# A hybrid decoder block: x fetched turned, its normalisation applied to the products, parameter vectors as one table

## The reference, cut to what matters

```python
def rms_norm(x, g):
    xf = x.astype(jnp.float32)
    y = xf * lax.rsqrt(jnp.mean(xf * xf, axis=-1, keepdims=True) + EPS)
    return (y * g.astype(jnp.float32)).astype(x.dtype)
...
        n = rms_norm(h, g_mix[i])
        proj = n @ w_in[i]
        z = proj[..., :SPLIT_Z]
        xbc = proj[..., SPLIT_Z:SPLIT_XBC]
        dt_raw = proj[..., SPLIT_XBC:SPLIT_DT]
        q = proj[..., SPLIT_DT:SPLIT_Q].reshape(bsz, s, SB_HEADS, SB_HEAD_DIM)
        ...
        gates = jax.nn.sigmoid(proj[..., SPLIT_V:])
```

## Time and profile before

| | |
|---|---|
| median, lowest, highest of three runs | 1225.63, 1223.95, 1225.75 us |
| span of the profiled execution | 1222.8 us (its own time is not given beside it) |
| PE busy | 1161.0 us, 95% |
| DVE, ACT, POOL busy | 302.0, 245.0, 235.6 us |
| DMA, whole span | 451.56 MB, mean 369 GB/s |
| mean granted clock of PE | 0.998 |

### The profile page before, as it was taken

How to read it: one execution, slowest core, us unless ns; L and a number is a source line. 1 busy time by engine, 2 the same in 40 slices (tenths; PEclk the granted TensorE clock), 3 DMA queues, 4 the chain that set the end, 5 groups by cost and what they waited for, 6 DMA issues and landing times.

```text
span 1222.8 us, 15282 instructions
## 1 busy us (share of the span) xinstructions
PE 1161.0 (95%) x6802; PEld 591.8 (48%) x6802; DVE 302.0 (25%) x463; ACT 245.0 (20%) x349; POOL 235.6 (19%) x206
## 2 busy tenths in 40 slices
PE   9999999999999999999999999989999998899996
PEld 9998878998433333333333333333333333333332
DVE  5448363224311221121122112111211211121112
ACT  6486686445101000000000000000000000000001
POOL 6979769882001000000000000000000000000000
PEclk9999999999999999999999999999999999999999
DMA  9644537848899999999999999999999999999994
GB/s 318 209 138 140 171 104 275 318 154 366 369 426 427 421 429 426 437 430 428 429 429 431 435 431 430 428 433 431 430 430 432 429 431 434 429 429 410 428 427 199
DMA packets 44702, 451.56 MB, mean 369 GB/s; under 512 B 4916, under 2 KB 5272, under 8 KB 27736
## 3 DMA queue, kind: packets, MB, share of 16 engines
q1 hardware_dynamic: 44632, 450.54, 88.8%
HBM read 449.48 MB, written 1.05 MB: 368 GB/s over the span
## 4 chain that ended last, share of the span: by engine, by line
PE 62%; DMA 33%; DVE 2%; ACT 1%; issue 1%; POOL 1%; DVEq 0%; ACTq 0%; POOLq 0%
DMA ring<-in_w_down 20%; PE ps L1275 19%; PE ps L1299 12%; PE ps L865 10%; DMA spare_quad<-in_w_down 7%; DMA kv_quad<-in_w_down 6%; PE ps L808 6%; PE ps L1246 3%; PE ps L1321 2%; PE ps L1178 2%; PE ps L829 1%; PE ps L1312 1%; PE ps L1197 1%; PE ps L980 1%; PE ps L889 0%
## 5 line engine op out<-in xcount | busy, mean ns | idle before, releaser
L513 POOL TENSOR_TENSOR w_parts<-ring,w_parts 128x512 fp32r<-128x512 f32 x162 | 216.9, 1373 | 42.0 <-ACT w_parts L1487 33.3
L692 POOL TENSOR_SCALAR ss<-ss 128x1 f32<-128x1 f32 (+2 forms) x8 | 1.5, 191 | 868.9 <-ACT junk L1477 864.5
L1275 PE MATMUL ps<-ring,xs 128*64 128x512 f32 x688 | 151.8, 595 | 5.8 <-DMA ring<-in_w_gu 5.8
L2216 DVE TENSOR_SCALAR xbuf<-ps 128x512 f32<-128x512 f32 x32 | 22.1, 691 | 526.4 <-PE ps L1275 526.4
L1299 PE MATMUL ps<-ring,xbuf 128*64 128x512 f32 x576 | 128.1, 595 | 17.0 <-DMA ring<-in_w_down 17.0
L1275 PE MATMUL ps<-ring,nT 128*64 128x512 f32 x560 | 123.5, 595 | 3.6 <-DMA ring<-in_w_gu 3.6
L1747 ACT ACTIVATE xbuf<-xbuf 128x512 f32<-128x512 f32 x32 | 20.2, 631 | 469.0 <-DVE xbuf L2216 469.0
L865 PE MATMUL ps<-w_parts,xT_hi 128*128 128x512 f32 x352 | 110.4, 395 | 0.0
L1275 PEld LDWEIGHTS ps<-ring,xs 128*64 128x64 f32 x688 | 47.9, 137 | 101.5 <-issue 90.3
L1487 ACT ACTIVATE w_parts<-ring 128x2048 fp32r<-128x2048 f32 x41 | 78.2, 1915 | 65.3 <-PE ps L865 39.4
L1299 PEld LDWEIGHTS ps<-ring,xbuf 128*64 128x64 f32 x576 | 43.9, 137 | 90.0 <-issue 85.2
(11 more groups left out here) (312 smaller groups left out, 1314.3 us busy)
## 6 DMA issues: line engine op xcount, KB each, us to landing
ring<-in_w_gu SPq DMA_DIRECT2D x24, 4096.0 KB, 41.5
ring<-in_w_gu SPq DMA_DIRECT2D x30, 2048.0 KB, 14.8
ring<-in_w_down SPq DMA_DIRECT2D x12, 4096.0 KB, 39.7
spare_quad<-in_w_gu SPq DMA_DIRECT2D x8, 4096.0 KB, 41.5
kv_quad<-in_w_gu SPq DMA_DIRECT2D x8, 4096.0 KB, 41.6
ring<-in_w_in SPq DMA_DIRECT2D x24, 1024.0 KB, 5.2
ring<-in_w_down SPq DMA_DIRECT2D x12, 2048.0 KB, 14.7
kv_quad<-in_w_gu SPq DMA_DIRECT2D x10, 2048.0 KB, 15.0
```

Source lines behind the costliest of these rows:

```text
L513: ops.tensor_tensor(w_lo[:, m % SPLIT, c], ring_slot(m)[:, c], w_hi[:, m % SPLIT, c], ALU.subtract).then_inc(lo_ready[name], 1)
L1275: i = mm(ps[64 * half:64 * half + 64, 4 + q, :], xg[:, k, (j % GE) * SLOTS:(j % GE + 1) * SLOTS], w[:, q * FF + half * 512:q * FF + half * ...
L2216: V.tensor_scalar(gl, ps[:, 4, :], LIM, None, ALU.min).then_inc(gl_ready, 1)
```

## The change

x comes in twice: once turned on the host, 128 partitions by 8 tiles by 256 tokens (`x_raw`, in two halves), and once as before (`h`), now behind chunk 2. The parts of x are made straight from `x_raw` and g_mix, without the root. The root is worked out beside the first products, and multiplied in afterwards: for the channel layout as a row over the tokens (`x_scale`, which two products on PE spread over the partitions behind chunk 2, in `scale_row`), for the token layout as a factor per partition when a stripe is emptied. q and k are emptied by DVE in place of ACT. The parameter vectors are one table laid out on the host (`columns`), fetched straight into `pcol`. Chunk 0 is fetched in two halves. POOL's root stands between its second and third tile of chunk 2.

```diff
-    s += [("q", "w_in", COL_Q, KD, "channel", "act"), ("k", "w_in", COL_K, KD, "channel", "act"),
+    s += [("q", "w_in", COL_Q, KD, "channel", "dve"), ("k", "w_in", COL_K, KD, "channel", "dve"),
...
-WARM = (18, 8, 4)
+WARM = (20, 4)
...
+            sp_.dma_start(pcol[:], columns).then_inc(prm_in, 16)
+            fetch_x(0)
             for m, (n, c) in enumerate(CHUNKS):
...
+                if m == 0:
+                    sp_.dma_start(dst[:, 0:LO_HALF], src[:, 0:LO_HALF]).then_inc(first_in, 16)
+                    sp_.dma_start(dst[:, LO_HALF:], src[:, LO_HALF:]).then_inc(slot_full[slot(m)], 16)
+                    fetch_x(1)
+                else:
+                    sp_.dma_start(dst, src).then_inc(slot_full[slot(m)], 16)
+                if m == 2:
+                    sp_.dma_start(h[:], x[0].rearrange("(b p) d -> p b d", p=P)).then_inc(x_in, 16)
...
+            low_part(pool, nc.gpsimd, "pool", 0, tiles=range(LO_HALF, KT))
+            low_part(pool, nc.gpsimd, "pool", LO_DVE, tiles=range(LO_HALF))
             root("x", 0, 2, D, 1)
-            low_part(pool, nc.gpsimd, "pool", 0, tiles=range(LO_HALF, KT))
-            for m in range(LO_DVE, 9):
+            low_part(pool, nc.gpsimd, "pool", LO_DVE, tiles=range(LO_HALF, KT))
+            for m in range(LO_DVE + 1, 9):
                 low_part(pool, nc.gpsimd, "pool", m)
...
+            def scale_row():
+
+                pe.wait_ge(consts, 5)
+                pe.wait_ge(rstd, 1)
+                for b in range(TB):
+                    i = mm(ps[:, 5, b * P:(b + 1) * P], ss[:, b:b + 1].broadcast_to([P, P]), ident[:],
+                           start=True, stop=True)
+                i.then_inc(row_done, 1)
+
             pe.wait_ge(consts, 2)
             ones_products(WARM[0])
-            pe.wait_ge(prm_in, 16 * 7)
...
-            pair_transposes(xn, (0, 1, 2, 3))
-            for n in range(3):
-                stripe(n, xT, tiles=x_lo if n == 0 else None)
+            pe.wait_ge(prm_in, 16)
+            stripe(0, xT)
+            stripe(1, xT, parts=(0,))
+            scale_row()
+            stripe(1, xT, parts=(1,))
+            stripe(2, xT)
...
+                if name in ("v", "z", "gate"):
+                    act.wait_ge(rstd, 1)
+                    for b in range(TB):
+                        ins = af(dst[:, b], src[:, b], func, scale=ss[:, b:b + 1])
+                    return ins.then_inc(stripe_out["act"], 1)
...
+            act.wait_ge(prm_in, 16)
+            x_high((2, 3))
             first_high((0, 1))
-            act.wait_ge(pcol_ready, 1)
-            high_tiles(TR_X, xT_hi, g_mix_k, (1,), x_hi)
             first_high((2, 3))
-            high_tiles(TR_X, xT_hi, g_mix_k, (2, 3), x_hi)
+            x_high((4, 5, 6, 7))
             splits_to(2)
+            act.wait_ge(x_in, 16)
+            squares(h[:, 0, :], 0)
             act.wait_ge(dtw_in, 64)
+            act.wait_ge(sq_done, SQUARED["x"])
             af(w_dt_hi[:], w_dt[:], ACT.Copy).then_inc(dt_hi, 1)
...
                 splits_to(products_done(n) + SPLIT - 1)
+                act.wait_ge(x_scaled, n + 1)
                 for cb in range(4):
...
-            empty(FIRST["q"], scale=DH ** -0.5)
-            empty(FIRST["k"])
+            splits_to(products_done(FIRST["k"]) + SPLIT - 1)
...
             for m in range(1, LO_DVE):
                 low_part(dve, V, "dve", m)
+            dve.wait_ge(x_in, 16)
+            squares(xn, h, 0)
+            dve.wait_ge(dt_hi, 1)
+            V.tensor_tensor(w_dt_lo[:], w_dt[:], w_dt_hi[:], ALU.subtract).then_inc(dt_lo, 1)
+            dve.wait_ge(row_done, 1)
+            step(V.tensor_copy(x_scale[:], ps[:, 5, 0:T]))
...
+            def scale_stripe(n):
+
+                src = channel_stripe(n)
+                V.tensor_tensor(src, src, x_row, ALU.mult).then_inc(x_scaled, 1)
...
             for c in range(NCB):
+                if c % 4 == 0:
+                    scale_stripe(c // 4)
                 convolve(c)
...
+            V.scalar_tensor_tensor(out=qT[:], in0=channel_stripe(FIRST["q"]), scalar=DH ** -0.5, in1=x_row,
+                                   op0=ALU.mult, op1=ALU.mult).then_inc(stripe_out["dve"], 1)
...
+            V.tensor_tensor(kT, channel_stripe(FIRST["k"]), x_row, ALU.mult).then_inc(stripe_out["dve"], 1)
```

More of the change, by code:

```diff
@@ L252, with build @@
 ROWS = ROW_FIN + KD
[L255 to L257 removed]
+def build(nc, x, x_turned, columns, mem, w_in, dt_bias, a_log, d_skip, w_ssd_out, w_sb_out, w_out, w_xq, w_xkv,
+          w_xo, g_moe, w_router, b_router, w_gu, b_gu, w_down, b_down, out):
     mats = {"w_in": w_in[0], "w_xkv": w_xkv[0], "w_ssd_out": w_ssd_out[0], "w_sb_out": w_sb_out[0],
@@ L573, in first_free, with fetch_x @@
                                                  if 2 * r + late == halves_pair(m)) + 1)
[L575 to L581, removed]
+            def fetch_x(half):
+                k = slice(4 * half, 4 * half + 4)
+                sp_.dma_start(x_raw[:, k, :], x_turned[:, k, :]).then_inc(xr_in[half], 16)
+            sp_.dma_start(pcol[:], columns).then_inc(prm_in, 16)
+            fetch_x(0)
             for m, (n, c) in enumerate(CHUNKS):
@@ L1882, in per_head @@
                 return head_rows[:, i, :].unsqueeze(1).broadcast_to([P, TB, H_SSD])
-            V.tensor_tensor(dt4[:, 0], ps[:, 4, 0:32].rearrange("p (b h) -> p b h", b=TB), per_head(0),
-                            ALU.add).then_inc(dt_raw, 1)
+            for b in range(TB):
+                i = V.scalar_tensor_tensor(out=dt4[:, 0, b], in0=ps[:, 4, b * H_SSD:(b + 1) * H_SSD],
+                                           scalar=ss[:, b:b + 1], in1=head_rows[:, 0, :], op0=ALU.mult, op1=ALU.add)
+            i.then_inc(dt_raw, 1)
             dve.wait_ge(dt_raw, 1)
@@ L2287, in _, with laid_out @@
                                        op0=ALU.mult, op1=ALU.mult).then_inc(out_ready, 1)
-_INS = ["x", "mem", "g_mix", "w_in", "conv_w", "conv_b", "dt_bias", "a_log", "d_skip", "g_ssd", "w_ssd_out",
-        "w_sb_out", "w_out", "g_xattn", "g_mem", "w_xq", "w_xkv", "w_xo", "g_moe", "w_router", "b_router",
-        "w_gu", "b_gu", "w_down", "b_down", "g_final"]
+_INS = ["x", "x_turned", "columns", "mem", "w_in", "dt_bias", "a_log", "d_skip", "w_ssd_out", "w_sb_out", "w_out",
+        "w_xq", "w_xkv", "w_xo", "g_moe", "w_router", "b_router", "w_gu", "b_gu", "w_down", "b_down"]
+def laid_out(inputs):
+    a = dict(inputs)
+    a["x_turned"] = np.asarray(inputs["x"])[0].T.reshape(KD, P, T).transpose(1, 0, 2)
+    rows = [np.asarray(inputs[n]).reshape(-1, P) for n in ("g_mix", "g_xattn", "g_mem", "g_ssd", "conv_w", "conv_b",
+                                                           "g_final")]
+    a["columns"] = np.concatenate(rows).T
+    return a
 def kernel(**inputs):
```

91 lines of the change are left out of this document (42 added, 49 removed).

## The result

The changed kernel takes 1231.93 us (median of 6 runs, 1229.57 to 1234.15) against 1225.62 for the kernel before on the same chip (6 runs, 1223.95 to 1225.86): ratio 1.0057, 95% interval 1.0047 to 1.0067, so 6.3 us more. The forecast was 2.1 more. The profiled executions span 1228.2 and 1222.8 us.

The account below looks back on a forecast made before the run. PE's gapless products bound the front, expert weight fetches the rest from about 600 us. Small tables cost +2.0 at stripe 2's start, later stripes +0.1: 1225.6 + 2.1 = 1227.7 us, range 1224.5 to 1230.3.

Parts of the forecast that it names:

- (a): Chunk 2: the second fetch of x delays POOL's later tiles; end at 26.9, undisturbed 25.3, leaving 2.5 of 4 us.
- the root: Ahead of POOL's third tile of chunk 2: h lands at 17.3, root ready 2.4 later, at 19.7.
- chunk 1 lands at 11.9 as before: Start of the fetch stream: table, turned x, chunk 0 and chunk 1 are the same 3 MB, so landing stays at 11.9.
- the price of the added megabyte: Fetch stream: 2.7 us per MB from the trace; the skill's table gave an estimate of 3.1.
- (c): From chunk 2's end: x row, copy, scaling, taps, convolution; stripe 2 may start at 35.8, hidden under 37.2.
- (b): Small tables behind 7 MB land at 25.2, delaying ACT's split; chunk 3 ends at 37.2, 2.0 later than 35.2.
- only the scaling chain binds: Rival at stripe 2's start: small tables overtake the stream, scaling remains; +0.3 to +1.0, 1226.4, chance 0.18 shared with small savings.
- the mark: Stripe 2's start at 35.2 in the kernel before; after it PE never waits for the front's start again.
- PE idle for about 4 us in chunk 3: Expected sign in chunk 3's first tiles: PE idle about 4 us, where there was no wait before.
- The slow clock: Rival at chunk 3's stall: PE's clock falls to half, at least 1.4 more; 1229.2, chance 0.25.
- The early start: Kernel start: first product near 7.1 instead of 11.35, PE at chunk 2 near 19.6, about 4 us early.

Follow-up runs that it names:

- the megabyte alone: The kernel before with one more 1 MB fetch of x behind chunk 2, unread, ACT's wait for the small tables covering it too; measured ratio 1.0031.

## Why the prediction was wrong

*The sign and the place were right,* though another step than the forecast one brought the cost. There is a cost at stripe 2 that reaches the end nearly unchanged (5.4 there, 7.0 with the clock's second fall, 6.3 in the medians). The size was wrong, and the binding step was the wrong one.

*The failed step is (a), chunk 2's end: 26.9 forecast, 31.3 measured.* The first term that was wrong is the root, ready at 22.7 and not at 19.7. The prediction took it from h alone, 17.3 + 2.4. h came at 18.6, which makes it 21.0. But POOL gets to the root only behind its first two tiles of chunk 2, and the sum has no term for them: even at their lone price of 2.5 they end at 20.6, which makes it 21.7. Beside DVE's sum they took 3.53 (and the sum 1.88 and not 1.22), which makes it 22.7. So 1.3 + 0.7 + 1.0 = 3.0, and tiles 2 and 3 came 3.0 later.

The late h doesn't come from the rate: 2.7 us per MB held (chunk 1 is split from 13.3, chunk 2 from 16.0, h is used from 18.6). It comes from "chunk 1 lands at 11.9 as before". The first 3 MB landed 1.4 later, and in the run without the halves h is there at 17.0. The second wrong term is the clock, which (a) put at nothing: 1.4 behind PE's waits in chunk 2. 3.0 + 1.4 = 4.4.

The Trainium skill, "SBUF — State Buffer", section "Who interferes with whom", says that a VectorE instruction with two SBUF inputs contends with a GpSimd instruction that reads SBUF. The trace agrees: 1.88 together, 1.22 alone, for the same instruction. The Trainium skill's rule in "DMA: Bandwidth & Descriptors", section "Bandwidth", to batch DMAs to at least 1 MiB, was quoted in the prediction only for the price of the added megabyte. It also spoke against the halves, and the trace agrees in direction: 246 and 313 GB/s with them, 392 and 407 without.

*Step (c), the scaling chain,* was forecast at 8.9 from chunk 2's end and measured at 40.59 - 31.3 = 9.3 (row 0.6 for 0.5, copy 0.42 for 0.3). The chain was right, but it hangs on (a); with (a) 4.4 late it passed (b). The rival "only the scaling chain binds" named the mechanism and gave it +0.3 to +1.0, because it too used 26.9. That moving the row alone takes stripe 2's start from 40.6 to 38.0, and 4.2 off the front with the clock's part, shows it.

*Step (b), the small tables:* 25.2 forecast, 26.02 measured; chunk 3 ended at 38.1 (37.2 forecast), which alone would have been +2.9 at the mark. Right as a mechanism, but hidden 2.3 us deep, and the sign that it named, PE idle for about 4 us in chunk 3, didn't come (0.36, since PE came there late itself). Moving the tables alone changed nothing, and they showed only once the root or the row was moved.

*The slow clock* was a rival at +1.4 or more for one place. It came at two others, within chunk 2 and behind the scaling chain, and cost about 2.7 together. It was no alternative to the forecast but an addition to a stall, as the megabyte alone shows too (2.2 + 1.7), though not to every one (none behind the 2.92 us).

*The early start:* 7.1 forecast, 8.68 measured, chunk 2 at 21.1 and not 19.6. By itself this made the front no later, since chunk 2 waited anyway.

*What stays open:* why halves of 512 KB run slower while the DMA engines are busy (share 0.95) is not explained; and why the clock falls behind some waits and not behind others of the same length. Of the 7.0 us at the w_dt products the runs give 2.7 to the clock; they don't split the other 4.3 uniquely, since root, row, halves and tables stand in one another's cover.

## What to carry to other kernels

Two chains that end within a microsecond or two of each other must both be priced with their inputs late: an error in a shared input (h) moves one past the other, and a fix of the one alone uncovers the next. When something is moved behind work to save a wait, place its consumer's consumer too; here four small products in a stall that was there anyway were worth 4 us, 1.6 of them in clock. And an instruction that is moved into an engine's queue waits for what stands ahead of it there, not only for its own input, as the root did for POOL's two tiles. Price a stall of the array with the clock behind it, and an instruction that runs beside another engine's by a row in which both run.
